# Rotary halves of the first block swapped by ScalarE copies instead of a permutation product

## The chip, the cores and the metric

One core of one Trainium2 chip. The metric is device microseconds (us) for one whole execution of the program. The names of the engines are those of the profile: PE is TensorE, PEld its weight loads, DVE is VectorE, ACT is ScalarE, POOL is GpSimd, SP issues the transfers of the weights.

## What is computed

Two transformer blocks, one after the other, each of two layers, in float32, on 256 tokens of width 1024. The part that the change touches is the projection of queries and keys of the first block's dilated attention and their rotary turn, and beside it on the same engines runs a gated recurrence (HGRN2):

```python
def apply_rope(x, cos, sin):
    x1, x2 = jnp.split(x, 2, axis=-1)
    return jnp.concatenate([x1 * cos - x2 * sin, x2 * cos + x1 * sin], axis=-1)

    z = h @ w_in[l]
    q_a, k_a, v_a, q_b, f_b, i_b, og_b, gate_a, gate_b = jnp.split(z, split_at, axis=-1)
    q_a = apply_rope(q_a.reshape(att_shape), cos, sin)      # 3 groups x 4 heads x 128
    k_a = apply_rope(k_a.reshape(att_shape), cos, sin)
    y_a = dilated_attention(q_a, k_a, v_a) @ w_att_branch[l]
    o_b = hgrn2_recurrence(...)
```

## The kernel before

Activations stand transposed: the 128 elements of a head lie on the 128 partitions, the 256 tokens along a row. So a rotary turn needs, for each head, the upper 64 partitions beside the lower 64 and the other way round.

All weights come as tiles of 128 x 2048 float32, streamed by SP into a ring of four buffers (`ring`). For each tile, ACT rounds it to `w_hi` (`high`, L246, three buffers) and DVE forms the rest `ring_lo` (`low`, L253); PE then multiplies high and low parts in three products for each pair (`triple`, L259), 48 products of 256 columns for a tile, into one of three PSUM banks. ACT copies the finished bank out (`evac`, L838) and at once does `high` for the tile three further on.

The order on every engine is written out by hand, and the engines meet by semaphores. The stage around the change is a loop of passes i = 0 to 8 in each of the two layers of the first block, with two tiles to a pass: tiles n = 2i and 2i + 1. Tiles 0 to 11 are queries and keys, tiles 12 to 17 values. Interleaved with them runs the recurrence in eight levels. One pass is, engine by engine:

- PE (`one_pe`): tile 2i, the rotation of tile 2i - 1, tile 2i + 1, the rotation of tile 2i, then `level(i)` (L638), 32 small products of `e_buf`. The rotation (`rotate`, L619) multiplies the evacuated tile `qk` by the permutation matrix `C_R1` (with its minus signs) into PSUM bank 3; it is a float32 product of 512 columns, which stands in the trace as two. `rotate(n)` waits until DVE has used up the bank's last content (`rot_scaled`).
- ACT (`one_act`): `decay(i)` (L853, an exponential), then for each of the two tiles `evac` and `high`.
- DVE (`one_dve`): `gather(i - 1)` (L1087), `rot_scale(2i - 2)` (L1097, rotated values times sine, into `rope_b`), `factors(i)` (L1072 and L1073, which release `level(i)` by `e_ready`), `args(i + 1)` (L1059 and L1063, which release `decay(i + 1)`), `low` for tile 2i + 3, `rot_scale(2i - 1)`, `low` for tile 2i + 4.
- POOL (`one_pool`): for each tile 0 to 11 the product with the cosine (L1285, into `rope_a`) and, once DVE has scaled the rotated values, the sum (L1289, back into `qk`), which counts `rope_done`.

The rotations, scalings and sums of a layer are twelve each. The attention after the loop waits for all twelve sums. Here and below, `tile n`, `rot_scale(n)` and so on are counted from the first tile of queries.

Of the kernel before, what the change touches and what calls it, by code (L numbers as in the profile page):

```python
# [25 lines left out]
ACT = mybir.ActivationFunctionType  # L26
ALU = mybir.AluOpType
AX = mybir.AxisListType

P = 128  # L30
T = 256
# [24 lines left out]
M_QK, M_V = MIX + 12, MIX + 24  # L56
# [11 lines left out]
HD = 64  # L68
# [36 lines left out]
C_ID, C_ONE, C_BD, C_R1, C_R2, C_TRI = (P * i for i in range(6))  # L105
# [24 lines left out]
def program(nc, x_t, mem_t, pos, stream, ada, vec, con, lmask, out):  # L130
    with ExitStack() as ctx:
        def sb(name, shape, dt=F32):
            return ctx.enter_context(nc.sbuf_tensor(name, shape, dt))
# [13 lines left out]
        qk = sb("qk", [P, 24, T])  # L147
# [14 lines left out]
        def at(name, shape, offset, dt=F32):  # L162
            return nc.alloc_sbuf_tensor_at(name, shape, dt, offset=offset)
# [13 lines left out]
        prob_2 = [at("prob_20", [P, 3 * P], hq_at), at("prob_21", [P, 3 * P], hq_at + 3 * P * 4)]  # L177
        rope_a = at("rope_a", [P, 2, T], prob_t_at)
        rope_b = at("rope_b", [P, 2, T], prob_t_at + 2 * T * 4)
        con_sb = sb("con_sb", [P, C_W])  # L180
        vec_sb = sb("vec_sb", [P, VEC_W])
        lm = sb("lm", [P, LEVELS, P], U8)
        cos1 = sb("cos1", [P, T])
        sin1 = sb("sin1", [P, T])
# [15 lines left out]
        ps = ctx.enter_context(nc.psum_tensor("ps", [P, 8, 512], F32))  # L200

        def C(at, n):
            return con_sb[:, at:at + n]
# [22 lines left out]
        S = type("S", (), s)  # L226
# [94 lines left out]
        def norm_act(act, chain, n, x_count, sq, src=x, between=None):  # L321
            for half in range(2):
                if x_count:
                    act.wait_ge(S.x_ready, x_count)
                nc.scalar.activation(sq[:, 4 * half:4 * half + 4, :], src[:, 4 * half:4 * half + 4, :],  # L325
                                     ACT.Square).then_inc(S.sq_ready, 1)
            if between:
                between()
            act.wait_ge(S.var_ready, n + 1)
            chain(nc.scalar.activation(rstd[:], var[:], ACT.Ln))  # L330
            nc.scalar.activation(rstd[:], rstd[:], ACT.Exp, scale=-0.5).then_inc(S.rstd_ready, 1)
# [174 lines left out]
        with nc.Block() as block:  # L506
            @block.sync
            def _(sp):
                sp.dma_start(con_sb[:], con[:, 0:C_W]).then_inc(S.load, 16)
                sp.dma_start(vec_sb[:], vec).then_inc(S.load, 16)  # L510
                sp.dma_start(pos_i[:], pos.broadcast_to([P, T])).then_inc(S.load, 16)
                sp.dma_start(e_buf[1][:].rearrange("p k t -> p (k t)")[:, 0:LEVELS * P], lmask).then_inc(S.load, 16)
                sp.dma_start(mem[:], mem_t.rearrange("(k p) t -> p k t", p=P)).then_inc(S.load, 16)
                sp.dma_start(x[:], x_t.rearrange("(k p) t -> p k t", p=P)).then_inc(S.load, 16)
                for j in range(RING):
                    sp.dma_start(ring[:, j, :], stream[j]).then_inc(loaded[j], 16)
                sp.wait_ge(S.load, 96)
# [11 lines left out]
            @block.scalar  # L529
            def _(act):  # L530
                chain = Chain(act, S.act_chain)
                act.wait_ge(S.load, 96)
                act.wait_ge(S.vec_ready, 1)
                norm_act(act, chain, 0, 0, e_buf[0], mem)

                act.wait_ge(S.decay_arg, 1)
                nc.scalar.activation(lb[:], lb[:], ACT.Exp).then_inc(S.decay_exp, 1)
                act.wait_ge(S.rot_scaled, 1)
                nc.scalar.activation(sin1[:], sin1[:], ACT.Sin)
                nc.scalar.activation(cos1[:], cos1[:], ACT.Sin)  # L540
                nc.scalar.activation(silu_c[:], vec_sb[:, VEC_C:VEC_C + KD], ACT.Silu)

# [58 lines left out]
        def one_pe(pe, l):  # L601
# [9 lines left out]
                    pe.wait_ge(S.evac_done, n - 2)  # L611
                (project_tok if n >= 8 else project)(pe, MIX + n, n % 3, h2)

            def rotate(n):

                pe.wait_ge(S.evac_done, 12 + n + 1)
                if n >= 1:
                    pe.wait_ge(S.rot_scaled, n)
                nc.tensor.matmul(ps[:, 3, :], C(C_R1, P), qk[:, 2 * n:2 * n + 2, :].rearrange("p k t -> p (k t)"),  # L619
                                 start=True, stop=True).then_inc(S.rot_done, 1)  # L620

            def level(i):

                if i < LEVELS:
# [18 lines left out]
            for i in range(LEVELS + 1):  # L643
                for n in (2 * i, 2 * i + 1):
                    pe.wait_ge(S.evac_done, 12 + n - 2)
                    (project if n < 12 else project_tok)(pe, M_QK + n, (12 + n) % 3, h2)
                    if 1 <= n <= 12:
                        rotate(n - 1)
                if i == LEVELS:
                    pe.wait_ge(S.cumsum_ready, 1)  # L650
                level(i)
# [9 lines left out]
            for hd in range(HG):  # L661
                if hd % 4 == 0:
# [4 lines left out]
                                 start=True, stop=False, skip_group_check=True)  # L667
# [6 lines left out]
            for b in range(4):  # L674
                if b % 2 == 0:
                    pe.wait_ge(S.o_copied, b // 2 + 1)
                mm = nc.tensor.matmul(ps[:, 4 + b, :], ones, hq[:, 2 * b:2 * b + 2, :].rearrange("p k t -> p (k t)"),
                                      start=True, stop=True)
# [41 lines left out]
            n = 5  # L720
# [22 lines left out]
            for j in range(2):  # L743
                p = M_YA + j
# [78 lines left out]
        def one_act(act, l):  # L823
# [24 lines left out]
            for n in range(1, 4):  # L848
                evac(M_I + n, hi[:, :, n * T:(n + 1) * T], (8 + n) % 3)

            def decay(i):
                act.wait_ge(S.decay_arg, i + 1)
                nc.scalar.activation(e_buf[i % 2][:], e_buf[i % 2][:], ACT.Exp).then_inc(S.decay_exp, 1)  # L853

            for i in range(LEVELS + 1):
                if i < LEVELS:
                    decay(i)
                for n in (2 * i, 2 * i + 1):
                    dst = qk[:, 2 * n:2 * n + 2, :] if n < 12 else val[:, :, (n - 12) * T:(n - 11) * T]
                    evac(M_QK + n, dst, (12 + n) % 3)  # L860

# [14 lines left out]
            for g in range(2):  # L876
                act.wait_ge(S.o_done, g + 1)
                act.wait_ge(S.level_done, 2 * LEVELS + 2)
                part = ps[:, 4 + 2 * g:6 + 2 * g, :].rearrange("p b (a t) -> p (b a) t", a=2)
# [28 lines left out]
            n = 5  # L908
# [13 lines left out]
            for k in range(KD):  # L922
                ins = nc.scalar.activation(mem_hi[:, k, :], mem[:, k, :], ACT.Copy,
                                           scale=v_now[:, V1_MEM + k:V1_MEM + k + 1])
# [68 lines left out]
        def one_dve(dve, l):  # L993
# [20 lines left out]
            for hd in range(HG):  # L1014
                ins = nc.vector.reciprocal(hk[:, hd, :], hk[:, hd, :])
# [6 lines left out]
            for hd in range(HG):  # L1022
                ins = nc.vector.tensor_scalar(hk[:, hd, :], hk[:, hd, :], lb_now[:, 0, hd:hd + 1],
                                              lb_now[:, 1, hd:hd + 1], ALU.mult, ALU.add)
# [67 lines left out]
            def rot_scale(n):  # L1092

                dve.wait_ge(S.rot_done, n + 1)
                if n >= 1:
                    dve.wait_ge(S.rope_done, n)
                nc.vector.tensor_tensor(rope_b[:], ps[:, 3, :].rearrange("p (a t) -> p a t", a=2),  # L1097
                                        sin1[:].unsqueeze(1).broadcast_to([P, 2, T]),
                                        ALU.mult).then_inc(S.rot_scaled, 1)

# [98 lines left out]
            for k in range(KD):  # L1199
                ins = nc.vector.scalar_tensor_tensor(out=mem_lo[:, k, :], in0=mem[:, k, :],  # L1200
                                                     scalar=v_now[:, V1_MEM + k:V1_MEM + k + 1],
                                                     in1=mem_hi[:, k, :].bitcast(F32), op0=ALU.mult, op1=ALU.subtract)
# [3 lines left out]
            for b in range(4):  # L1206
                dve.wait_ge(S.tile_done, M_YB + b + 1)
                part = e_buf[0][:, 2 * b:2 * b + 2, :].rearrange("p k t -> p (k t)")
# [4 lines left out]
            for j in range(2):  # L1213
                dve.wait_ge(S.tile_done, M_YA + j + 1)
                part = e_buf[1][:, 4 * j:4 * j + 4, :].rearrange("p k t -> p (k t)")
# [53 lines left out]
        def one_pool(pool, l):  # L1269
            def free_a(i):  # L1270
                pool.wait_ge(S.h_ready, 2) if i == 0 else pool.wait_ge(S.ss_ready, 1)

            def free_b(i):
                pool.wait_ge(S.h_ready, 8) if i == 0 else pool.wait_ge(S.ss_ready, 4)

            ada_pool(pool, l, 0, 0, free_a)
            pool.wait_ge(S.x_ready, 4)
            nc.gpsimd.memset(a_hg[:], 0.0).then_inc(S.a_zeroed, 1)

            for n in range(12):  # L1280
                part = qk[:, 2 * n:2 * n + 2, :]
                pool.wait_ge(S.evac_done, 12 + n + 1)
                if n >= 1:
                    pool.wait_ge(S.rope_done, n)
                nc.gpsimd.tensor_tensor(rope_a[:], part, cos1[:].unsqueeze(1).broadcast_to([P, 2, T]),  # L1285
                                        ALU.mult).then_inc(S.pool_chain, 1)
                pool.wait_ge(S.pool_chain, n + 1)
                pool.wait_ge(S.rot_scaled, n + 1)
                nc.gpsimd.tensor_tensor(part, rope_a[:], rope_b[:], ALU.add).then_inc(S.rope_done, 1)  # L1289

            ada_pool(pool, l, PER_FFN, PER_FFN, free_b)

# [748 lines left out]
```

## Time and profile before

| | us |
|---|---|
| runs | 3351.6, 3361.8, 3361.89 |
| their median | 3361.8 |
| the profiled execution | 3350.6 |
| its span, first to last instruction | 3348.9 |
| PE busy | 3020.6 (90%) |
| DVE busy | 2167.7 (65%) |
| ACT busy | 1274.7 (38%) |
| POOL busy | 179.2 (5%) |

The mean granted TensorE clock of the profiled execution is 0.946 of full speed. The loop of the change runs in layer one from about 350 to 506 us, in layer two from about 1323 to 1479 us. A busy share is a mean over stages with different limits; what a change in a stage is worth shows in the timeline of that stage: which engine waits there, and for whom. An instruction's duration in the timeline includes some 0.1 us that overlaps the next one's, so costs are best read from one start to the next.

### The profile page before, as it was taken

How to read it: one execution, taken by the hardware profiler on the slowest of the kernel's cores; microseconds unless marked ns; L12 is line 12 of the kernel's file. 1: busy time of each engine (PE TensorE's matmuls, PEld its weight loads, DVE VectorE, ACT ScalarE, POOL GpSimd, SP SyncE). 2: the span in 40 equal slices, each digit the busy share in tenths (PEclk: the TensorE clock that was granted, in tenths of full speed). 3: DMA queues.
4: the chain of work that ended last, by engine and by line, in shares of the span. 5: the costliest groups of instructions: out<-in, count | busy, mean ns of one | idle time of the engine just before them, and what ended most of it. 6: DMA issues, size and time to landing. Idle time of an engine off the chain costs nothing. (4 is left out here: it accounts for less than half of the span.)

```text
span 3348.9 us, 54348 instructions
## 1 busy us (share of the span) xinstructions
PE 3020.6 (90%) x23240; PEld 2916.7 (87%) x23240; DVE 2167.7 (65%) x2739; ACT 1274.7 (38%) x1163; POOL 179.2 (5%) x173
## 2 busy tenths in 40 slices
PE   4998999998998989998988989988789889887899
PEld 4998998997998989898988979977589889776899
DVE  5666875554666667856546657666656576666566
ACT  3333434443323324344433333325523233255232
POOL 0000220000000000400000000001000000020000
PEclk8998999999998989999999989988889999888899
DMA  4663433443655644332535645633146556331464
GB/s 169 243 228 125 139 126 114 146 169 118 239 209 199 242 151 177 126 126 101 177 124 197 240 152 220 243 129 114 38 169 239 197 201 246 134 112 51 151 244 172
DMA packets 79821, 560.75 MB, mean 167 GB/s; under 512 B 8544, under 2 KB 11872, under 8 KB 12128
## 3 DMA queue, kind: packets, MB, share of 16 engines
q1 hardware_dynamic: 66912, 464.99, 38.6%
q0 software_dynamic: 12672, 92.28, 7.2%
q8 instruction: 188, 3.08, 0.4%
q14 instruction: 49, 0.40, 0.0%
HBM read 556.18 MB, written 1.05 MB: 166 GB/s over the span
## 5 line engine op out<-in xcount | busy, mean ns | idle before, releaser
L259 PE MATMUL ps<-h_hi,w_hi 128*128 128x256 f32 x4688 | 1360.2, 290 | 129.5 <-DVE h_lo L373 107.1
L253 DVE TENSOR_TENSOR ring_lo<-ring,w_hi 128x2048 fp32r<-128x2048 f32 x438 | 1007.9, 2303 | 714.2 <-ACT w_hi L246 707.2
L259 PE MATMUL ps<-h_lo,w_hi 128*128 128x256 f32 x4688 | 1341.7, 286 | 0.0
L259 PE MATMUL ps<-h_hi,ring_lo 128*128 128x256 f32 x4688 | 1340.9, 286 | 0.0
L246 ACT ACTIVATE w_hi<-ring 128x2048 fp32r<-128x2048 f32 x438 | 836.0, 1910 | 771.5 <-PE ps L259 642.1
L259 PEld LDWEIGHTS ps<-h_hi,w_hi 128*128 128x128 f32 x4688 | 915.7, 195 | 146.9 <-DVE h_lo L373 115.0
L259 PEld LDWEIGHTS ps<-h_lo,w_hi 128*128 128x128 f32 x4688 | 916.0, 195 | 6.7 <-issue 6.4
L259 PEld LDWEIGHTS ps<-h_hi,ring_lo 128*128 128x128 f32 x4688 | 914.7, 195 | 0.0
L259 PE MATMUL ps<-g_hi,w_hi 128*128 128x256 f32 x1408 | 398.5, 283 | 0.0
L259 PE MATMUL ps<-g_lo,w_hi 128*128 128x256 f32 x1408 | 398.5, 283 | 0.0
L259 PE MATMUL ps<-g_hi,ring_lo 128*128 128x256 f32 x1408 | 398.4, 283 | 0.0
L259 PEld LDWEIGHTS ps<-g_hi,w_hi 128*128 128x128 f32 x1408 | 270.3, 192 | 0.0
L259 PEld LDWEIGHTS ps<-g_lo,w_hi 128*128 128x128 f32 x1408 | 270.3, 192 | 0.0
L259 PEld LDWEIGHTS ps<-g_hi,ring_lo 128*128 128x128 f32 x1408 | 270.3, 192 | 0.0
L432 DVE SCALAR_TENSOR_TENSOR val<-e,silu_c,val 128x256 f32<-128x256 f32 x528 | 216.3, 478 | 0.0
L458 ACT ACTIVATE g_f<-ps 128x512 f32<-128x512 f32 x88 | 52.6, 598 | 377.3 <-PE ps L259 377.3
L418 POOL DMA_DIRECT2D e<-ada x88 | 46.9, 533 | 2487.0 <-DVE h_lo L373 1271.4
L337 PE MATMUL ps<-e,con_sb 128*128 128x256 f32 x256 | 87.6, 516 | 79.4 <-ACT e L325 79.4
L337 PEld LDWEIGHTS ps<-e,con_sb 128*128 128x128 f32 x256 | 67.9, 272 | 95.1 <-ACT e L325 68.2
L259 PE MATMUL ps<-w_hi,h_hi 128*128 128x256 f32 x448 | 129.1, 288 | 0.0
L259 PE MATMUL ps<-w_hi,h_lo 128*128 128x256 f32 x448 | 126.7, 283 | 0.0
L259 PE MATMUL ps<-ring_lo,h_hi 128*128 128x256 f32 x448 | 126.7, 283 | 0.0
(300 smaller groups left out, 3195.1 us busy)
## 6 DMA issues: line engine op xcount, KB each, us to landing
ring<-stream SPq DMA_DIRECT2D x438, 1024.0 KB, 4.8
e<-ada POOLq DMA_DIRECT2D x88, 1024.0 KB, 5.1
con_sb<-con SPq DMA_DIRECT2D x1, 1024.0 KB, 5.0
mem<-mem_t SPq DMA_DIRECT2D x1, 1024.0 KB, 10.1
x<-x_t SPq DMA_DIRECT2D x1, 1024.0 KB, 12.6
out_t<-x SPq DMA_DIRECT2D x1, 1024.0 KB, 4.4
con_sb<-con SPq DMA_DIRECT2D x1, 640.0 KB, 4.0
e<-lmask SPq DMA_DIRECT2D x1, 512.0 KB, 7.9
```

Source lines behind the costliest of these rows:

```text
L246: nc.scalar.activation(w_hi[:, p % HIGHS, :], ring[:, p % RING, :], ACT.Copy).then_inc(S.w_hi_ready, 1)
L253: nc.vector.tensor_tensor(ring_lo[:, p % RING, :], ring[:, p % RING, :], w_hi[:, p % HIGHS, :].bitcast(F32), ALU.subtract).then_inc(S.w_lo ...
L259: mm = nc.tensor.matmul(out, a, b, start=start and n == 0, stop=stop and n == 2, skip_group_check=group)
L337: mm = nc.tensor.matmul(ps[:, 0, 0:T], ones, sq[:, k, :], start=(k == 0), stop=(k == KD - 1))
L418: pool.dma_start(e_buf[(i + 1) % 2][:].rearrange("p k t -> p (k t)"), ada[bass.ds(l * (2 * PER_FFN) + (first + i), 1)].rearrange("o p n -> ...
L432: ins = nc.vector.scalar_tensor_tensor(out=sums[k % 2], in0=w[:, k, :], scalar=c, in1=sums[k % 2], op0=ALU.mult, op1=ALU.add)
L458: nc.scalar.activation(g_f[:, i % 2, :], ps[:, i % 2, :], ACT.Silu).then_inc(S.silu_done, 1)
```

## The change

It removes the twelve permutation products of a layer. Instead, before each evacuation of a query or key tile, ACT copies the two halves of the PSUM bank crosswise: partitions 64 to 127 to partitions 0 to 63 of a buffer in SBUF, and 0 to 63 to 64 to 127 (`turn`). The buffer is one of two (`turned`), of which one is the old `rope_b`. `turn(n)` waits for the tile, and from n = 2 on also until POOL has summed tile n - 2, since it writes that tile's buffer. The minus sign of the matrix moves into the sine table, whose lower 64 partitions are now made with a scale of -1. DVE scales in place, from SBUF instead of PSUM, and no longer waits for POOL.

```diff
--- before.py
+++ after.py
@@ -177,6 +177,7 @@
         prob_2 = [at("prob_20", [P, 3 * P], hq_at), at("prob_21", [P, 3 * P], hq_at + 3 * P * 4)]
         rope_a = at("rope_a", [P, 2, T], prob_t_at)
         rope_b = at("rope_b", [P, 2, T], prob_t_at + 2 * T * 4)
+        turned = [rope_b, sb("turned1", [P, 2, T])]
         con_sb = sb("con_sb", [P, C_W])
         vec_sb = sb("vec_sb", [P, VEC_W])
         lm = sb("lm", [P, LEVELS, P], U8)
@@ -536,7 +537,8 @@
                 act.wait_ge(S.decay_arg, 1)
                 nc.scalar.activation(lb[:], lb[:], ACT.Exp).then_inc(S.decay_exp, 1)
                 act.wait_ge(S.rot_scaled, 1)
-                nc.scalar.activation(sin1[:], sin1[:], ACT.Sin)
+                nc.scalar.activation(sin1[0:HD, :], sin1[0:HD, :], ACT.Sin, scale=-1.0)
+                nc.scalar.activation(sin1[HD:P, :], sin1[HD:P, :], ACT.Sin)
                 nc.scalar.activation(cos1[:], cos1[:], ACT.Sin)
                 nc.scalar.activation(silu_c[:], vec_sb[:, VEC_C:VEC_C + KD], ACT.Silu)
 
@@ -611,14 +613,6 @@
                     pe.wait_ge(S.evac_done, n - 2)
                 (project_tok if n >= 8 else project)(pe, MIX + n, n % 3, h2)
 
-            def rotate(n):
-
-                pe.wait_ge(S.evac_done, 12 + n + 1)
-                if n >= 1:
-                    pe.wait_ge(S.rot_scaled, n)
-                nc.tensor.matmul(ps[:, 3, :], C(C_R1, P), qk[:, 2 * n:2 * n + 2, :].rearrange("p k t -> p (k t)"),
-                                 start=True, stop=True).then_inc(S.rot_done, 1)
-
             def level(i):
 
                 if i < LEVELS:
@@ -644,8 +638,6 @@
                 for n in (2 * i, 2 * i + 1):
                     pe.wait_ge(S.evac_done, 12 + n - 2)
                     (project if n < 12 else project_tok)(pe, M_QK + n, (12 + n) % 3, h2)
-                    if 1 <= n <= 12:
-                        rotate(n - 1)
                 if i == LEVELS:
                     pe.wait_ge(S.cumsum_ready, 1)
                 level(i)
@@ -848,6 +840,17 @@
             for n in range(1, 4):
                 evac(M_I + n, hi[:, :, n * T:(n + 1) * T], (8 + n) % 3)
 
+            def turn(n):
+
+                act.wait_ge(S.tile_done, M_QK + n + 1)
+                if n >= 2:
+                    act.wait_ge(S.rope_done, n - 1)
+                for a, b in ((0, HD), (HD, 0)):
+                    ins = nc.scalar.activation(turned[n % 2][a:a + HD, :, :],
+                                               ps[b:b + HD, (12 + n) % 3, :].rearrange("p (a t) -> p a t", a=2),
+                                               ACT.Copy)
+                ins.then_inc(S.rot_done, 1)
+
             def decay(i):
                 act.wait_ge(S.decay_arg, i + 1)
                 nc.scalar.activation(e_buf[i % 2][:], e_buf[i % 2][:], ACT.Exp).then_inc(S.decay_exp, 1)
@@ -856,6 +859,8 @@
                 if i < LEVELS:
                     decay(i)
                 for n in (2 * i, 2 * i + 1):
+                    if n < 12:
+                        turn(n)
                     dst = qk[:, 2 * n:2 * n + 2, :] if n < 12 else val[:, :, (n - 12) * T:(n - 11) * T]
                     evac(M_QK + n, dst, (12 + n) % 3)
 
@@ -1092,9 +1097,7 @@
             def rot_scale(n):
 
                 dve.wait_ge(S.rot_done, n + 1)
-                if n >= 1:
-                    dve.wait_ge(S.rope_done, n)
-                nc.vector.tensor_tensor(rope_b[:], ps[:, 3, :].rearrange("p (a t) -> p a t", a=2),
+                nc.vector.tensor_tensor(turned[n % 2][:], turned[n % 2][:],
                                         sin1[:].unsqueeze(1).broadcast_to([P, 2, T]),
                                         ALU.mult).then_inc(S.rot_scaled, 1)
 
@@ -1286,7 +1289,7 @@
                                         ALU.mult).then_inc(S.pool_chain, 1)
                 pool.wait_ge(S.pool_chain, n + 1)
                 pool.wait_ge(S.rot_scaled, n + 1)
-                nc.gpsimd.tensor_tensor(part, rope_a[:], rope_b[:], ALU.add).then_inc(S.rope_done, 1)
+                nc.gpsimd.tensor_tensor(part, rope_a[:], turned[n % 2][:], ALU.add).then_inc(S.rope_done, 1)
 
             ada_pool(pool, l, PER_FFN, PER_FFN, free_b)
 
```

On ACT, two tiles of the loop in layer one, with what each instruction waits for. Before (`qk<-ps` is the evacuation, `w_hi<-ring` is `high`, `e<-e` is `decay`):

```order
L853 ACTIVATE e<-e 128x2048 [waits decay_arg]
L838 ACTIVATE qk<-ps 128x512 [waits tile_done]
L237 REGISTER_ALU [waits tile_done]
L246 ACTIVATE w_hi<-ring 128x2048 [waits slot_loaded0]
L838 ACTIVATE qk<-ps 128x512 [waits tile_done]
L246 ACTIVATE w_hi<-ring 128x2048 [waits slot_loaded1,tile_done]
```

The same place in the changed program:

```order
L856 ACTIVATE e<-e 128x2048 [waits decay_arg]
L849 ACTIVATE rope_b<-ps 64x512 [waits rope_done,tile_done]
L849 ACTIVATE rope_b<-ps 64x512
L830 ACTIVATE qk<-ps 128x512 [waits tile_done]
L238 REGISTER_ALU [waits tile_done]
L247 ACTIVATE w_hi<-ring 128x2048 [waits slot_loaded0]
L849 ACTIVATE turned<-ps 64x512 [waits rope_done,tile_done]
L849 ACTIVATE turned<-ps 64x512
L830 ACTIVATE qk<-ps 128x512 [waits tile_done]
L247 ACTIVATE w_hi<-ring 128x2048 [waits slot_loaded1,tile_done]
```

Each evacuation has two copies ahead of it, and the first of them waits for POOL's `rope_done`; the evacuation and `high` stand behind that wait.

On PE, between the last product of a tile, its neighbour's rotation and a level, before:

```order
L259 MATMUL ps<-h_hi,ring_lo 128x256
L619 MATMUL ps<-qk,con_sb 128x512 [waits rot_scaled,evac_done]
L638 MATMUL ps<-e 128x128 [waits level_used,e_ready]
L638 MATMUL ps<-e 128x128 x7
L638 MATMUL ps<-e 128x128 [waits level_used]
L638 MATMUL ps<-e 128x128 x7
```

In the changed program the level's own instructions are:

```order
L632 MATMUL ps<-e 128x128 [waits level_used,e_ready]
L632 MATMUL ps<-e 128x128 x7
L632 MATMUL ps<-e 128x128 [waits level_used]
L632 MATMUL ps<-e 128x128 x7
```

The product L619 is gone from PE, and with it PE's waits for `rot_scaled`; the level still waits for DVE's `e_ready`.

## Rows read from the trace of the kernel before

**Rows 1.** The page, part 1: busy time of each engine and its share.

```profile
PE 3020.6 (90%) x23240; PEld 2916.7 (87%) x23240; DVE 2167.7 (65%) x2739; ACT 1274.7 (38%) x1163; POOL 179.2 (5%) x173
```

**Rows 2.** Windows, one pass: length, busy PE PEld DVE ACT POOL, clock, DMA share, GB/s.

```profile
421.40:439.00 17.60, 17.02 (x135) 15.88 (x134) 15.57 (x13) 6.60 (x5) 6.79 (x4) 1.00 0.34 120
```

**Rows 3.** Waits, 360 to 480 us: who waited for whom, total us, times, longest.

```profile
DVE ring_lo L253 <- ACT w_hi L246: 17.2, 8, 3.3
...
PE ps L619 <- DVE rope_b L1097: 2.4, 3, 1.2
```

**Rows 4.** Timeline of ACT: start us, us, engine, line, [idle before <- releaser].

```profile
360.38 0.60 ACT L838 ACTIVATE qk<-ps 128x512 f32<-128x512 f32 x1 [3.36 <-PE ps L259]
...
439.20 0.60 ACT L838 ACTIVATE qk<-ps 128x512 f32<-128x512 f32 x1 [6.80 <-PE ps L259]
...
445.80 0.60 ACT L838 ACTIVATE qk<-ps 128x512 f32<-128x512 f32 x1 [4.20 <-PE ps L259]
446.29 1.90 ACT L246 ACTIVATE w_hi<-ring 128x2048 fp32r<-128x2048 f32 x1
...
463.43 0.60 ACT L838 ACTIVATE val<-ps 128x512 f32<-128x512 f32 x1 [4.20 <-PE ps L259]
...
472.76 0.60 ACT L838 ACTIVATE val<-ps 128x512 f32<-128x512 f32 x1 [5.13 <-PE ps L259]
...
478.52 0.60 ACT L838 ACTIVATE val<-ps 128x512 f32<-128x512 f32 x1 [3.36 <-PE ps L259]
...
487.84 0.60 ACT L838 ACTIVATE val<-ps 128x512 f32<-128x512 f32 x1 [6.93 <-PE ps L259]
```

**Rows 5.** Timeline of DVE, layer one.

```profile
375.75 0.68 DVE L1097 TENSOR_TENSOR rope_b<-ps,sin 128x512 f32<-128x512 f32 x1
...
427.92 0.68 DVE L1097 TENSOR_TENSOR rope_b<-ps,sin 128x512 f32<-128x512 f32 x1
...
433.51 2.59 DVE L1087 COPY_PREDICATED a_hg<-lm,ps 128x512 f32<-128x512 uint8 x4
...
436.60 1.20 DVE L1072 TENSOR_TENSOR e<-e,hk 128x1024 f32<-128x1024 f32 x1
437.73 2.30 DVE L1073 TENSOR_TENSOR e<-e,hq 128x1024 f32<-128x1024 f32 x1
439.96 2.32 DVE L1059 TENSOR_TENSOR e<-hb 128x1024 f32<-128x1024 f32 x1
...
443.34 2.28 DVE L253 TENSOR_TENSOR ring_lo<-ring,w_hi 128x2048 fp32r<-128x2048 f32 x1
445.54 0.68 DVE L1097 TENSOR_TENSOR rope_b<-ps,sin 128x512 f32<-128x512 f32 x1
448.23 2.97 DVE L253 TENSOR_TENSOR ring_lo<-ring,w_hi 128x2048 fp32r<-128x2048 f32 x1 [2.01 <-ACT w_hi L246]
...
471.68 1.22 DVE L1073 TENSOR_TENSOR e<-e,hq 128x1024 f32<-128x1024 f32 x1
```

**Rows 6.** Timeline of POOL, the same stretch.

```profile
436.81 2.14 POOL L1289 TENSOR_TENSOR qk<-rope_a,rope_b 128x512 f32<-128x512 f32 x1 [5.38 <-DVE rope_b L1097]
439.10 2.10 POOL L1285 TENSOR_TENSOR rope_a<-qk,cos 128x512 f32<-128x512 f32 x1
446.36 1.27 POOL L1289 TENSOR_TENSOR qk<-rope_a,rope_b 128x512 f32<-128x512 f32 x1 [5.16 <-DVE rope_b L1097]
```

**Rows 7.** Groups by line and shape, whole span: busy us, mean ns | idle before.

```profile
L1577 ACT ACTIVATE qk<-qk 64x256 f32<-64x256 f32 x2 | 0.8, 414 | 6.9 <-POOL qk L1853 6.9
...
L343 DVE TENSOR_TENSOR e<-e 128x512 f32<-128x512 f32 x16 | 11.1, 692 | 0.5
```

**Rows 8.** PE after an idle stretch: timeline, then windows (length, busy PE, clock, DMA).

```profile
537.68 0.77 PE L691 MATMUL ps<-qk 128*128 128x128 f32 x2 [3.09 <-ACT hi L886]
...
537.00:538.00 1.00, 0.32 (x1) 0.50 1.05 442
...
542.00:543.00 1.00, 1.00 (x7) 0.50 0.00 0
```

## Prediction

> **What bounds the kernel now.** The busy shares come first: PE works 90% of the span, DVE 65%, ACT 38%, POOL 5% [rows 1]. That says where to look, not what this stage waits for. So next the windows: in one pass of the loop, 17.60 us long, PE is busy 17.02 us, DVE 15.57 us, ACT 6.60 us and POOL 6.79 us, at full granted clock [rows 2]. PE is the bound, DVE is only 2 us behind it, and ACT has room by its sum alone. The waits of the stage name what little is lost: PE's rotations wait 2.4 us for the scaling on DVE, in three waits, and DVE waits 17.2 us in all for ACT's `high` [rows 3]. Last the timelines, with which the order of the handovers can be followed.
>
> ACT's evacuations mark the ends of the tiles. With a rotation between them two tiles are 445.80 - 439.20 = 6.60 us apart, without one 478.52 - 472.76 = 5.76 us, so a rotation holds PE for 0.84 us. A pass without rotations takes 487.84 - 472.76 = 15.08 us [rows 4]; two tiles of 5.76 us leave 3.56 us for the level. A pass with them is 445.54 - 427.92 = 17.62 us, read from one odd `rot_scale` to the next [rows 5].
>
> **What is removed.** 12 rotations in each layer, 24 x 0.84 = 20.2 us of PE, and the waits before them, 2 x 2.4 = 4.8 us. All of it lies on PE's path, so 25.0 us is what the change gives back if nothing else comes last.
>
> **What is added, first the copies.** 24 copies of 64 x 512 a layer on ACT. The trace has no such copy. The full evacuation of 128 x 512 lasts 0.60 us, and the next instruction starts 0.49 us after it [rows 4]; an activation of 64 x 256 takes 0.414 us [rows 7], much more than half of that for a quarter of the elements, so half the partitions save nothing. I take 0.49 us from start to start, 0.98 us a tile; the ends are half of 0.49 us (cost by elements) and the undivided 0.60 us. The busy sum of ACT rises to 6.60 + 1.96 = 8.6 us a pass, far below 17.6. By sums alone they are hidden.
>
> **Then the order, on which the forecast rests.** `turn(n)` may not write before POOL has summed tile n - 2. Take n = 11, an odd tile. The sum of tile 9 needs `rot_scale(9)`, which stands late in DVE's pass and starts at 445.54 [rows 5]; the sum starts at 446.36 and lasts 1.27 us [rows 6], to 447.63. But tile 11 ends at 445.80 [rows 4]. So even in the old timing ACT would stand still for 1.8 us at `turn(11)`, and behind that wait are the copies, the evacuation and `high(14)`. For `high(14)` waits DVE's very next instruction, `low(14)`. This closes a ring that did not exist before: `rot_scale(2i-1)`, sum, `turn(2i+1)`, evacuation, `high(2i+4)`, `low(2i+4)`, the whole next DVE pass, `rot_scale(2i+1)`. Its length, from start to start:
> - `rot_scale` to the start of the sum, 446.36 - 445.54 = 0.82; the sum 1.27 [rows 5, 6]
> - handover to ACT, an estimate of 0.10; two copies 0.98; evacuation 446.29 - 445.80 = 0.49; `high` 1.90; handover to DVE, 448.23 - 448.19 = 0.04 [rows 4, 5]. Up to here 5.60
> - `low`, 445.54 - 443.34 = 2.20; it took 2.97 us where a POOL instruction ran at its start, and POOL will by then be idle
> - the rest of the DVE pass, from `gather` at 433.51 to the next odd `rot_scale` at 445.54: 12.03 [rows 5]
>
> That is 5.60 + 2.20 + 12.03 = 19.83 us against 17.62 us now. PE needs only 15.08 us of it and must wait about 4.75 us for `e_ready` in each pass. ACT's other waits are not last: `turn(2i+2)`, in the same pass, waits for the sum behind `rot_scale(2i)`. Counted from the start of `factors`, 436.60, that sum ends after 2.35 us (436.81 + 2.14) [rows 6]; handover, copies, evacuation and `high` take 3.5 us more, and DVE asks for the result after 443.34 - 436.60 = 6.74 us [rows 5], so 0.9 us is to spare.
>
> Inside the 12.03 us are two slow instructions. `factors`' second product takes 2.30 us with POOL at work and 1.22 us in the last pass, where POOL is idle [rows 5]; POOL's sum, 1.27 us alone, takes 2.14 us beside DVE [rows 6]. They exclude each other: the one that comes second waits out the first. The Trainium skill says so (SBUF — State Buffer, Who interferes with whom): a VectorE instruction with two SBUF inputs and a GpSimd instruction that reads SBUF take one shared port, and the second "fully blocks". By that rule, with which the trace agrees, the scaling is exposed for the first time, since its first input moves from PSUM to SBUF; a collision would add up to 1.27 us to each of 24. I add nothing, because POOL has no work ready when a scaling starts. By itself the scaling stays as it is: 0.68 us from PSUM [rows 5], 0.69 us for the same size from SBUF [rows 7].
>
> **The sum for a layer.** `turn(1)` delays `low(4)` and all after it by 0.98 us: `rot_scale(1)` starts at 375.75 + 0.98 = 376.73 [rows 5]. Four rings of 19.83 us bring `rot_scale(9)` to 456.05. The ring's first part (5.60), `low` (2.20), and from `gather` to the end of `factors` (437.73 + 2.30 - 433.51 = 6.52) release level 6 at 470.4. Before, that level started when tile 13 ended, 463.4 [rows 4]. So each layer loses 7.0 us; the rotations and waits taken off PE are already in it, for they only lengthen PE's new wait. From pass 7 on there is neither a rotation nor a turn, PE runs through in both kernels, and the 7.0 us stays. Two layers: +14.0 us.
>
> **The clock.** After 3.09 us of idling PE ran at a granted clock of 0.50, which is the 1.2 GHz level, from 537.68 to beyond 543 us [rows 8], so it lost half of some 5.8 us, 2.9 us. The new waits are longer, 4.75 us. Within the ring such a loss is covered: PE then waits 2.9 us less. Only after the last wait, at level 6, does it reach the end. I take 2.0 us a layer, with bounds 0 and 2.9: +4.0 us.
>
> The `Sin` of the setup becomes two instructions, once, some 0.4 us [rows 7]; I leave it out. No transfer is moved on a queue, and a slower pass asks for weights later than now. Sum: +14.0 + 4.0 = **+18.0 us**.
>
> The profiled execution took 3350.6 us, so it would be 3368.6. The four executions shown are two near 3351 and two near 3362, with the profiled one at the bottom, 11 us under the median. I cannot tell which of the two the next runs fall to, and forecast from their middle, 3356.5: **3374.5 us**. Bounds: with copies at half price, six times 0.49 us less in a layer (the entry, four rings, the exit) and no clock loss, +8.2 us on 3350.6 gives 3359; with copies at 0.60, the clock at 2.9 and 0.1 us more at each handover, +24 us on 3362 gives 3386.
>
> **The rivals.**
> - *The wait for the sum is never last* (faster). If DVE reached the odd scaling and POOL its sum before the tile two further on is ready, PE would keep its 25.0 us: 3356.5 - 25.0 = 3331.5. For it: POOL is busy 5% of the span, and the buffers are doubled. Against it: the two starts above, 445.54 and 445.80, and a PE that comes earlier without its rotations makes it worse. It would need the scaling some 2 us earlier in DVE's pass. Chance 0.08.
> - *POOL's collisions go away* (no change). If its two instructions no longer met `factors` and `args`, a ring would be 2.2 us shorter, 17.6 us, as the pass is now. With the same at the entry and exit level 6 would start about 5 us earlier than before, less a clock loss of about 1 us: -8 us for two layers, 3348. Against it: that sum still starts 0.2 us behind `factors`, since the scaling releases both, as now [rows 5, 6]. Chance 0.05.
> - *The idle PE becomes the bound again* (slower still). If each wait costs more than the 4.75 us that cover it, thus over 9.5 us of work at half clock, passes grow beyond 19.83. At 12 us, 1.25 us more in eight rings, +10 us: 3384.5. The low stretch seen was 5.8 us. Chance 0.07.
> - *It does not do what it says*, for instance the rotations still run. The order of instructions speaks against it; no change, 0.02.
>
> **How the numbers follow.** The forecast's case has 0.78. A measurement of this kernel can tell about 0.3%, 10 us, from no change; the forecast's lower bound lies under that, and 0.09 of its chance with it. Slower: 0.69 + 0.07 = 0.76. Within: 0.09 + 0.05 + 0.02 = 0.16. Faster: 0.08. The range 3350 to 3388 holds the forecast's own range, 3359 to 3386, most of the third rival and a part of the second; it leaves out the first.
>
> **What would show it.** ACT idle before the odd `turn` with `rope_done`, POOL's sum, as releaser, about 2 us after the scaling began; DVE idle about 5.0 us before every second `low` instead of 2.0; odd scalings 19.8 us apart; PE idle 4 to 5 us before levels 3 to 6, at a clock of 0.50 behind it; level 6 some 7 us later. If instead odd turns wait for PE alone, the forecast is wrong and the first rival holds. If the ring closes but is shorter than 17.6 us, my prices of its parts are wrong.

## The result, and the profile after

| | median us | executions | ratio to before, with its 95% interval |
|---|---|---|---|
| before | 3358.5 | 3350.7 to 3361.9 | |
| the change | 3384.2 | 3380.4 to 3384.8 | 1.0078 [1.0061, 1.0095] |
| forecast | 3374.5 | range 3350 to 3388 | slower, 0.76 |

One more execution of the changed kernel took 10123 us at a mean granted clock of 0.464 and is left out of the comparison; half the clock could at most double a time, so what tripled it is not shown. The change costs 0.78%, some 26 us. The profiled execution took 3380.4 us, its span is 3378.6 us, at a mean granted clock of 0.939 against 0.946.

The page, part 1 (busy time and share of each engine), of the changed kernel, beside [rows 1]:

```profile
PE 3022.9 (89%) x23192; PEld 2926.9 (87%) x23192; DVE 2162.9 (64%) x2739; ACT 1303.1 (39%) x1212; POOL 181.0 (5%) x173
```

There are 48 matmuls fewer on PE and 49 instructions more on ACT, and no engine is busier by more than 29 us. PE's own busy time has risen by 2 us although 20 us of products left it, because the same work is in part done at a lower clock (below). So the busy times do not say where the time went. The window of one pass does (columns as in [rows 2]):

```profile
417.80:437.80 20.00, 17.98 (x151) 17.78 (x151) 14.82 (x13) 8.96 (x9) 6.78 (x4) 0.99 0.31 106
```

A pass takes 20 us where it took 17.6, and both PE and DVE now have idle time in it: DVE is busy 14.82 us of 20, and PE 17.98, of which some belongs to work that it did late, after a wait and at half the clock. Since no engine is full here, a chain across engines must set the pass. The waits of the stage, 360 to 480 us, name its links (columns as in [rows 3]):

```profile
DVE ring_lo L254 <- ACT w_hi L247: 29.4, 6, 5.2
ACT rope_b L849 <- POOL qk L1292: 28.4, 5, 6.0
ACT turned L849 <- POOL qk L1292: 25.3, 5, 5.1
...
PE ps L632 <- DVE e L1078: 17.5, 5, 4.7
```

ACT waits for POOL's sums (both buffers), DVE for ACT's `high`, PE for DVE's `factors`. The lines on ACT and PE did not exist before; DVE's wait for `w_hi` was 17.2 us [rows 3]. One turn of the ring in the timelines of DVE, POOL and ACT, beside [rows 4 to 6]:

```profile
417.86 0.68 DVE L1100 TENSOR_TENSOR turned<-turned,sin 128x512 f32<-128x512 f32 x1
423.71 2.29 DVE L254 TENSOR_TENSOR ring_lo<-ring,w_hi 128x2048 fp32r<-128x2048 f32 x1 [5.17 <-ACT w_hi L247]
425.92 2.59 DVE L1092 COPY_PREDICATED a_hg<-lm,ps 128x512 f32<-128x512 uint8 x4
...
437.90 0.68 DVE L1100 TENSOR_TENSOR turned<-turned,sin 128x512 f32<-128x512 f32 x1
...
470.23 2.30 DVE L1078 TENSOR_TENSOR e<-e,hq 128x1024 f32<-128x1024 f32 x1
```

```profile
418.68 1.29 POOL L1292 TENSOR_TENSOR qk<-rope_a,turned 128x512 f32<-128x512 f32 x1 [5.16 <-DVE turned L1100]
420.12 1.30 POOL L1288 TENSOR_TENSOR rope_a<-qk,cos 128x512 f32<-128x512 f32 x1
```

```profile
420.07 1.20 ACT L849 ACTIVATE turned<-ps 64x512 f32<-64x512 f32 x2 [5.05 <-POOL qk L1292]
421.29 0.60 ACT L830 ACTIVATE qk<-ps 128x512 f32<-128x512 f32 x1
421.78 1.90 ACT L247 ACTIVATE w_hi<-ring 128x2048 fp32r<-128x2048 f32 x1
...
483.83 0.60 ACT L830 ACTIVATE val<-ps 128x512 f32<-128x512 f32 x1 [6.01 <-PE ps L260]
```

Follow the times: scaling 417.86, sum 418.68 to 419.97, copies 420.07, evacuation 421.29, `high` 421.78 to 423.68, `low` 423.71 after 5.17 us of idling, `gather` 425.92, and the next odd scaling at 437.90. The turn is 20.04 us.

A measure that serves for every kernel below is the **loop time**: from the start of ACT's evacuation of the last tile before the loop to that of tile 14, from where on no rotary work is left. It is 125.4 and 125.3 us in the two layers before (347.40 to 472.76 in layer one) and 135.6 us in each after (348.26 to 483.83). So the two loops cost 20.4 us of the 26.

### The profile page after: what moved, and what is told of

It is laid out like the page before. It is cut to its first block and busy times, and to the rows that moved or that the text cites. A ratio compares the mean times of both kernels' runs of the same rounds, so it can differ in the third digit from the quotient of the medians.

```text
span 3378.6 us, 54277 instructions
## 1 busy us (share of the span) xinstructions
PE 3022.9 (89%) x23192; PEld 2926.9 (87%) x23192; DVE 2162.9 (64%) x2739; ACT 1303.1 (39%) x1212; POOL 181.0 (5%) x173
## 5 line engine op out<-in xcount | busy, mean ns | idle before, releaser
L260 PE MATMUL ps<-w_hi,h_hi 128*128 128x256 f32 x448 | 128.2, 286 | 0.0
```

What stands on the lines that cost most here:

```text
L260: mm = nc.tensor.matmul(out, a, b, start=start and n == 0, stop=stop and n == 2, skip_group_check=group)
```

## The experiments

Ratios are to the kernel before, run beside each on the same chip, where its median was 3358.4, 3356.9 or 3360.2 us. Differences between two changed kernels are taken from their ratios, unless the same chip is named. The two kernels profiled again have one execution each.

| kernel | median us | ratio, interval | loop time (us), layers one and two |
|---|---|---|---|
| before, profile again | 3352.8 | | 125.4, 125.4 |
| change, profile again | 3380.4 | | 135.6, 135.7 |
| third buffer | 3327.3 | 0.9913 [0.9899, 0.9926] | 111.0, 111.0 |
| third buffer, again | 3328.9 | 0.9917 [0.9895, 0.9938] | 111.0, 111.0 |
| `high` first | 3330.1 | 0.9922 [0.9908, 0.9935] | 111.2, 111.0 |
| early scaling | 3342.8 | 0.9962 [0.9944, 0.9979] | 120.4, 120.4 |
| third buffer and product | 3350.2 | 0.9979 [0.9968, 0.9989] | 121.2, 121.2 |
| copies alone | 3363.6 | 1.0022 [1.0013, 1.0032] | 128.2, 128.2 |
| change and product | 3378.9 | 1.0067 [1.0054, 1.0081] | 135.6, 135.5 |
| change, copies doubled | 3401.4 | 1.0132 [1.0103, 1.0160] | 145.8, 145.7 |

**A third buffer.** The view that serves as third buffer is the part of `val` that tile 17 fills; its evacuation then waits for all sums.

```diff
-        turned = [rope_b, sb("turned1", [P, 2, T])]
+        turned = [rope_b, sb("turned1", [P, 2, T]), val[:, :, 5 * T:6 * T]]
...
-                if n >= 2:
-                    act.wait_ge(S.rope_done, n - 1)
-                for a, b in ((0, HD), (HD, 0)):
-                    ins = nc.scalar.activation(turned[n % 2][a:a + HD, :, :],
+                if n >= 3:
+                    act.wait_ge(S.rope_done, n - 2)
+                for a, b in ((0, HD), (HD, 0)):
+                    ins = nc.scalar.activation(turned[n % 3][a:a + HD, :, :],
...
+                    if n == 17:
+                        act.wait_ge(S.rope_done, 12)
```

DVE and POOL index the buffers by `n % 3` in the same way.

> The change with a third buffer for the swapped halves: turn(n) then waits for POOL's sum of tile n - 3 instead of n - 2. Theory (the ring scaling - sum - copies - evacuation - high - low - next DVE pass sets 20.03 us a pass): the odd turn now waits for an even sum, which is long done, the ring is open, odd scalings fall from 20.0 to about 15.5 us apart, and the time is about 26 us under the kernel before (24 rotations of 0.84 us and their waits gone), near 3330. Rival (the copies on ACT, or the scaling from SBUF, cost the time, whatever waits): it stays at the change's time, about 26 us over the kernel before.

Measured: 3327.3 us, 0.9913 of before, and 3328.9 us in the repetition. The same copies, the same scaling from SBUF, one buffer more, and 55 us less than the change. In ACT's timeline every turn now waits for PE alone:

```profile
415.11 1.20 ACT L849 ACTIVATE val<-ps 64x512 f32<-64x512 f32 x2 [3.91 <-PE ps L260]
416.34 0.60 ACT L830 ACTIVATE qk<-ps 128x512 f32<-128x512 f32 x1
416.83 1.91 ACT L247 ACTIVATE w_hi<-ring 128x2048 fp32r<-128x2048 f32 x1
420.87 1.20 ACT L849 ACTIVATE rope_b<-ps 64x512 f32<-64x512 f32 x2 [2.13 <-PE ps L260]
```

And on DVE the `low` that had waited 5.17 us follows the scaling almost at once:

```profile
423.75 0.68 DVE L1103 TENSOR_TENSOR turned<-turned,sin 128x512 f32<-128x512 f32 x1
424.52 2.29 DVE L254 TENSOR_TENSOR ring_lo<-ring,w_hi 128x2048 fp32r<-128x2048 f32 x1
...
438.84 0.68 DVE L1103 TENSOR_TENSOR rope_b<-rope_b,sin 128x512 f32<-128x512 f32 x1
```

The pass is 438.84 - 423.75 = 15.09 us, which is PE's own 15.08. The ring is the cause; the rival, that the copies or the scaling cost the time, falls. The window of this pass (columns as in [rows 2]) shows one thing more:

```profile
423.75:438.84 15.09, 15.09 (x130) 15.09 (x130) 15.00 (x13) 8.97 (x10) 8.95 (x4) 1.00 0.39 137
```

PE is full, but DVE is busy 15.00 of the 15.09 us as well, so by these numbers a further cut on PE alone would find DVE in its place.

The repetition stands beside the kernel with the product put back where the ring is open, on the same chip:

> The kernel with three buffers once more, on the same chip as the one with the product put back. The loops last 111.0 us each as before, against 125.4 us in the kernel before; the time is 26 to 30 us under the kernel before.

**`high` first.** The two buffers stay, and so does ACT's wait. Only `high` moves ahead of it.

```diff
                     if n < 12:
+                        high(act, l, 1, M_QK + n + HIGHS)
                         turn(n)
...
-                    evac(M_QK + n, dst, (12 + n) % 3)
+                    evac(M_QK + n, dst, (12 + n) % 3, ahead=n >= 12)
```

(`ahead` tells `evac` whether to do `high` behind it.)

> The change with two buffers, but ACT does high for the tile three further on before the two copies and not after the evacuation. Copies and their wait for the sum stay. Theory: low no longer stands behind the wait, the ring is open, and the time is about 26 us under the kernel before, as with a third buffer. Rival (what costs is the wait itself, or the number of ACT instructions): no gain over the change, 26 us over the kernel before.

Measured: 3330.1 us, 0.9922, equal to the third buffer within the intervals. Its ACT timeline:

```profile
419.32 1.91 ACT L247 ACTIVATE w_hi<-ring 128x2048 fp32r<-128x2048 f32 x1 [0.81 <-PE ps L260]
426.79 1.20 ACT L850 ACTIVATE turned<-ps 64x512 f32<-64x512 f32 x2 [5.55 <-POOL qk L1294]
...
434.41 1.91 ACT L247 ACTIVATE w_hi<-ring 128x2048 fp32r<-128x2048 f32 x1 [0.35 <-PE ps L260]
442.32 1.20 ACT L850 ACTIVATE turned<-ps 64x512 f32<-64x512 f32 x2 [6.00 <-POOL qk L1294]
```

ACT still idles 5.55 us for the sum, longer than the 5.05 us of the change, and the loops last 111.2 and 111.0 us, where they last 111.0 with the third buffer. So the wait's length is not the price; what stands behind it is.

It is not quite free either. The odd turns are 442.32 - 426.79 = 15.53 us apart, where PE needs 15.08 us a pass, and ACT's idle time before the odd `high` shrinks from pass to pass (0.81 us, then 0.35 us). What still stands behind the wait is `decay`, and DVE now waits for it:

```profile
430.45 2.21 DVE L1079 TENSOR_TENSOR e<-e,hk 128x1024 f32<-128x1024 f32 x1 [1.76 <-ACT e L857]
```

So a second ring goes through `decay` and `factors`, with a turn of 15.53 us. The loop ends before PE feels it; a loop of more passes might not, which was not tried.

**The product put back into the change.**

```diff
                     (project if n < 12 else project_tok)(pe, M_QK + n, (12 + n) % 3, h2)
+                    if 1 <= n <= 12:
+                        nc.tensor.matmul(ps[:, 3, :], C(C_R1, P), con_sb[:, C_OWN:C_OWN + 2 * T], start=True, stop=True)
```

> The change with a float32 product of 512 columns put back on PE after each of the tiles 1 to 12, as long as the old rotation; its result is used by nothing. Theory (PE waits about 5 us a pass in the changed kernel): 24 products of 0.84 us go into that idle time, the time is that of the change within 3 us. Rival (PE's path sets the end): 20 us more than the change.

Measured: 3378.9 us, ratio 1.0067 against the change's 1.0078, the intervals overlap, and the loops last 135.6 and 135.5 us as in the change. PE's waits before the levels fall from 17.5 to 8.9 us in layer one, so the products went into them. What the change takes off PE is worth nothing there, because PE waits anyway.

**The same product put back where the ring is open**, in the kernel with the third buffer.

> The change with the third buffer (ring open) and the unused product of 512 columns put back on PE after each of the tiles 1 to 12. Theory: now PE's path sets the pass, so each product costs its 0.84 us, 24 of them 20 us over the kernel with three buffers, about 3347, some 10 us under the kernel before, whose waits before the rotations stay away. In the changed kernel the same products cost nothing. Rival (the product costs nothing here either, the gain of the third buffer comes only from the waits on ACT): 3327.

Measured: 3350.2 us against 3328.9 us without it on the same chip, 21 us for 24 products, and the loops are 121.2 - 111.0 = 10.2 us longer each. Twelve times 0.84 us is 10.1. The same instructions cost 20 us or nothing, by what comes last in the pass. And the loops are still 4.1 us shorter each than those of the kernel before, which has the same products and waits before them. PE's listed waits before its rotations in layer one are 2.4 us for DVE and 0.7 us for ACT, 3.1 us together; where the other 1.0 us comes from was not looked into.

**The copies alone, in the kernel before**, into a part of `val` that is unused then, rotation by PE kept.

```diff
+                    if n < 12:
+                        act.wait_ge(S.tile_done, M_QK + n + 1)
+                        for a, b in ((0, HD), (HD, 0)):
+                            nc.scalar.activation(val[a:a + HD, :, (2 + n % 4) * T:(3 + n % 4) * T],
+                                                 ps[b:b + HD, (12 + n) % 3, :].rearrange("p (a t) -> p a t", a=2),
+                                                 ACT.Copy)
```

> The kernel before, with 24 copies of 64 x 512 a layer added on ACT at the places of the change, into a part of val that nothing uses then; rotation by PE and its buffers as before, no wait for POOL. Theory: without the wait the copies cost little, high comes 1.2 us later and PE's wait before a rotation grows by as much in the passes where it waits: 0 to 7 us over the kernel before. Rival (the copies themselves make the change slow): 20 us or more over it.

Measured: 1.0022, and 2.9 us a loop, 5.8 us in both. That is small but not nothing: `high` comes 1.2 us later, and with it DVE's `low` and the scaling for which PE's next rotation waits. These waits of PE for DVE in layer one rise from 2.4 to 5.8 us.

**The copies doubled, in the change.** Two more of them ahead of the two of each tile, into the same part of `val`, behind the same wait.

> The change with two more copies of 64 x 512 on ACT ahead of the two of each tile, behind the same wait, into a part of val that nothing uses then. Theory: they lie in the ring, so each of its turns is 1.2 us longer, odd scalings 21.2 us apart instead of 20.0, and six times 1.2 us a layer add 14 to 15 us to the time of the change, 41 us over the kernel before. Rival (ACT has slack, and only the wait matters): nothing is added. Rival (each ACT instruction counts at its cost): 24 x 1.2 = 29 us are added.

Measured: 3401.4 us, 1.0132, so 18 us over the change, and 10.2 us more in each loop. The direction and the place are confirmed, the size is above the 14 to 15 us. Odd scalings of the doubled kernel, and the even `low` ahead of one:

```profile
422.12 0.68 DVE L1104 TENSOR_TENSOR turned<-turned,sin 128x512 f32<-128x512 f32 x1
...
441.73 2.29 DVE L254 TENSOR_TENSOR ring_lo<-ring,w_hi 128x2048 fp32r<-128x2048 f32 x1 [0.52 <-ACT w_hi L247]
443.94 0.68 DVE L1104 TENSOR_TENSOR turned<-turned,sin 128x512 f32<-128x512 f32 x1
...
465.78 0.69 DVE L1104 TENSOR_TENSOR turned<-turned,sin 128x512 f32<-128x512 f32 x1
```

They are 21.8 us apart, where 20.03 + 1.22 = 21.25 was expected. The missing 0.6 us is the even turn: it had 0.9 us to spare by the prediction, less 0.24 us for the real price of two copies, and 1.22 us more takes that up and 0.56 us beyond. The row of the even `low` shows it, with 0.52 us of idling for `high` where the change has none. With 1.22 us at the entry and five turns of about 1.8 us the loop comes to the measured 10.2 us.

**The scaling of the odd tile moved ahead.**

```diff
                 if 0 <= 2 * i - 2 < 12:
                     rot_scale(2 * i - 2)
+                    rot_scale(2 * i - 1)
...
-                if 0 <= 2 * i - 1 < 12:
-                    rot_scale(2 * i - 1)
```

> The change with two buffers, but DVE scales the odd tile right after the even one, ahead of factors, and not after args and low. Theory of the ring: the sum of the odd tile comes about 10 us earlier in the pass, the wait of the odd turn is nearly gone, and the pass must shorten from 20.0 us. But POOL's four instructions of a pass then all meet factors and args on DVE, and each meeting costs DVE up to 1.3 us, so DVE itself needs 17.5 to 18 us without any idle time: the time of the kernel before within 5 us. Rival (the ring alone counts, meetings do not): a pass of 15 to 15.5 us, 26 us under the kernel before. Rival (no ring): the change's time.

Measured: 3342.8 us, 0.9962, some 13 us under the kernel before and 39 under the change. The ring is shorter, and what now sets the pass of 16.98 us (418.13 to 435.11) is DVE without a gap:

```profile
418.13 0.68 DVE L1100 TENSOR_TENSOR turned<-turned,sin 128x512 f32<-128x512 f32 x1
418.73 2.31 DVE L1077 TENSOR_TENSOR e<-e,hk 128x1024 f32<-128x1024 f32 x1
420.96 2.32 DVE L1078 TENSOR_TENSOR e<-e,hq 128x1024 f32<-128x1024 f32 x1
423.20 2.28 DVE L1064 TENSOR_TENSOR e<-hb 128x1024 f32<-128x1024 f32 x1
425.41 2.29 DVE L1068 TENSOR_TENSOR e<-hb 128x1024 f32<-128x1024 f32 x1
427.62 4.48 DVE L254 TENSOR_TENSOR ring_lo<-ring,w_hi 128x2048 fp32r<-128x2048 f32 x2
...
435.11 0.67 DVE L1100 TENSOR_TENSOR turned<-turned,sin 128x512 f32<-128x512 f32 x1
```

All four products of `factors` and `args` now take 2.3 us, where two of them took 1.2 [rows 5]: POOL's four instructions follow each other directly and meet all four. Expected was a pass of 17.5 to 18 us with up to 1.3 us a meeting; it is 8.89 us for the four from start to start, against 6.74 us before (436.60 to 443.34), so the two additional meetings cost 1.1 us each. The rival that knows only the ring (15 to 15.5 us) falls, and so does mine that it would end level with the kernel before.

**Both kernels profiled once more.**

> The kernel before once more, with its own profile. The loops of the change must last the same in each execution; if the clock falls after some idle stretches of the attention in one execution and not in the other, the times outside the loops differ by several us, and that is the spread of 3350 to 3363 us between executions.

> The changed kernel once more, with its own profile. The loops last as in its first profile, 20.03 us a pass, some 20 us more than before in both layers. If what it lost beyond these 20 us in its first profile is the clock after idle stretches elsewhere, that part has another size here.

The loop times repeat within 0.2 us. Outside the loops the profiles differ. From ACT's evacuation of tile 14 to its first instruction on `mem` behind the attention the kernel before took 142.3 and 139.4 us in layers one and two (142.8 and 139.4 in its second profile), the change 142.3 and 145.3 us, and 142.5 and 142.8 us in its second. The extra 5.9 us of the first pair in layer two stand behind idle stretches of PE that both kernels have: 2.7 us behind the first of them and 2.8 us behind the second. The first stretch, and a window of 5 us around its end (21.2 us later after the change), of PE alone, in the kernel before:

```profile
1510.72 0.46 PE L691 MATMUL ps<-qk 128*128 128x128 f32 x2 [3.09 <-ACT hi L886]
...
1510.00:1515.00 5.00, 4.28 (x31) 1.00 0.39 164
```

and the changed kernel:

```profile
1531.95 0.76 PE L683 MATMUL ps<-qk 128*128 128x128 f32 x2 [3.09 <-ACT hi L891]
...
1531.20:1536.20 5.00, 4.25 (x14) 0.50 0.37 157
```

The same 3.09 us of idling, nearly the same busy time, half the clock, and 14 matmuls instead of 31. The kernel before kept full clock behind that stretch and the changed one did not.

Over the whole span the first pair of profiles differs by 29.6 us, of which 9.2 lie outside the loops, and the second pair by 27.5 us, of which 7.0 do. The medians leave less, 25.7 - 20.4 = 5.3 us, because both profiles of the kernel before (3350.6 and 3352.8 us) fell among the fastest of its executions, which reach from 3350 to 3365 us. Nor is the place fixed: in the first pair 5.9 us stand in the attention of layer two, 2.5 us behind it and 0.9 us ahead of the first loop; in the second pair 3.4 us stand in that attention, 4.2 us behind it and 2.0 us between the two layers, and 2.6 us are gained earlier.

## Why the prediction was right, and where its sizes were off

**Sign and mechanism were right.** Each link of the ring stands in the profile at the place that was named. ACT waits for POOL's sum before every turn from n = 2 on; the odd turn starts at 420.07, 2.2 us after the scaling; DVE idles 5.17 us before `low` (5.0 foretold, 2.0 before); odd scalings are 20.03 us apart (19.83 foretold). Opening the ring by a third buffer or by the order on ACT removed all of the loss, and putting the product back changed nothing.

One sign came only in part. PE was to idle 4 to 5 us before each of the levels 3 to 6; it idled 4.66, 2.02, 4.68 and 3.27 us (and 2.87 us before level 2). PE alone in windows around the ends of the waits before levels 3 and 4:

```profile
412.00:417.00 5.00, 4.55 (x21) 0.50 0.03 11
...
431.00:436.00 5.00, 3.52 (x31) 1.00 0.66 213
```

Behind 4.66 us of idling the clock was at half, PE ran late, and its next wait was 2.6 us shorter, 2.02 us; behind that one the clock stayed full and the next wait was long again. This is the cover that the prediction argued with, and scalings 20.03 us apart in spite of it show that it held.

**The term of the ring.** Mis-sized was the copy: 0.49 us from start to start was taken from the evacuation. The row says 420.07 to 421.29, 1.22 us for two, so 0.61 each: the copies lie end to end and overlap nothing. That is 0.24 us more at six places of a layer, 1.4 us. All other parts of the 19.83 us were right to 0.05 us. The forecast loss of a loop without the clock, 7.0 us, becomes 8.4; measured are 8.2, since level 6 is released 472.53 - 348.26 = 124.27 us after the start of the loop and came at 463.43 - 347.40 = 116.03 us before.

**The clock after level 6.** Taken as 2.0 us a layer. `factors` ends at 470.23 + 2.30 = 472.53, tile 14 is evacuated at 483.83, 11.30 us later; at full clock that stretch takes 472.76 - 463.43 = 9.33 us [rows 4]. The cost is 1.97 us. In the eight loops of four profiles with the closed ring (the change twice, the product put back, the copies doubled) it is 1.88 to 1.98 us, so it repeats. The prediction had chosen 2.0 between bounds of 0 and 2.9 without working it out, so that it fits so closely is partly luck. The windows of PE at that place (length, busy PE, clock, DMA):

```profile
471.00:472.00 1.00, 0.00 (x0) 1.00 0.56 221
472.00:473.00 1.00, 0.42 (x2) 0.84 1.00 426
473.00:474.00 1.00, 1.00 (x7) 0.50 0.59 246
...
475.00:476.00 1.00, 1.00 (x7) 0.50 0.00 0
476.00:477.00 1.00, 1.00 (x11) 0.95 0.00 0
```

The loops have no other loss than the ring and this exit. Loop by loop, 8.2 + 2.0 = 10.2 us against 9.0 foretold.

**What the prediction did not have** is the rest: 26 us measured, 20.4 in the loops. The term that the sum put at nothing is the clock behind the idle stretches of the attention and of the second block. Their lengths stay, but whether the clock falls behind each is not the same from kernel to kernel, and by the medians the change came out 5 us worse there. The profiles show this for the attention of layer two; the other kernels went both ways, by comparing their ratios with their loops: the doubled copies lose some 4 us outside the loops, the early scaling gains about 3. That it follows from the shift in time was not tested by moving the stretches alone, so it stays an explanation. It also bears on the centre of the forecast: 3374.5 was 18 us over a middle of 3356.5. The middle was right to 2 us (the kernel before had a median of 3358.5), the 18 should have been 26, and 2.4 of the 8 us lie in the loops.

**The rivals.** "The wait for the sum is never last" did not happen. Its price was somewhat low: 25.0 us was said to be the gain, and with the third buffer the two loops are 2 x 14.3 = 28.6 us shorter than before (the time is 3327 to 3330 us, where 3331.5 was said). The products were priced right, 10.2 us a layer; the waits before them were worth 4.1 us a layer and not 2.4. "POOL's collisions go away" did not happen, `factors`' second product and `args`' first still take 2.3 us. "The idle PE becomes the bound again" did not happen; the stretches of half clock stay within PE's wait, as the rows of levels 3 and 4 show.

## What to carry to other kernels

Ask of a double buffer in which order its user and its releaser come on each engine, not how busy they are. Here the release of a buffer stood late in DVE's pass, the wait for it stood early on ACT, and ahead of the very instruction that DVE wanted next: three harmless orders that close into one ring. A wait costs what is queued behind it; moving one independent instruction ahead of the wait was worth as much as another buffer, some 52 us against the change. Look then for what is still queued behind it, here `decay`. And before paying for relief of the busiest engine, put the removed work back as a dummy: if nothing changes, something else comes last.

With the third buffer, or with `high` first, the idea of the change gives what the sum of instructions says, and a little more: 0.9913 of the kernel before, the fastest version here.

## What the runs showed of the hardware that was not expected

Copies of 64 x 512 from PSUM on ACT that cross from one half of the partitions to the other last 0.60 us, as one of 128 x 512 does, but the next instruction starts only 0.61 us after each, against 0.49 us after the evacuation. Why they don't overlap was not tried.

DVE's products with two SBUF inputs and POOL's instructions held each other up wherever the rows show them meeting. In the kernel with early scaling every one of the four met: each took 2.3 us instead of 1.2, and POOL's took 2.1 us instead of 1.3 (the first 1.6). The exposure of the in-place scaling, which the prediction foresaw, cost nothing in the change: it stayed at 0.68 us, since POOL had no work ready then. With the third buffer the two did meet, and the even scaling took 0.73 us, since POOL's product reached 0.19 us into it:

```profile
413.03 1.31 POOL L1291 TENSOR_TENSOR rope_a<-qk,cos 128x512 f32<-128x512 f32 x1
...
414.15 0.73 DVE L1103 TENSOR_TENSOR rope_b<-rope_b,sin 128x512 f32<-128x512 f32 x1
```
